# Latent attention on one core: VectorE copies the first tile's turned probabilities, and output products of finished heads are placed between the last steps

## What is computed

```
for j in range(S // Q_BLOCK):                       # 4 query tiles of 128 rows, S = 512
    L = (j + 1) * Q_BLOCK
    s = (q_nope[tile j] . k_nope[:L] + q_pe[tile j] . k_pe[:L]) * scale    # 16 heads
    p = softmax(where(causal_mask(...), s, NEG_INF))
    outs.append(einsum('bhqk,bkhd->bqhd', p, v[:, :L]))
o = concatenate(outs).reshape(B, S, 16 * 64)
x = x + g_m * (o @ w_o)                             # w_o is 1024 x 1024
x = x + g_f * hier_moe(...)                         # 32 experts, top 2 of one group
```

## Time and profile before

| | us |
|---|---|
| median of 3 runs | 1137.25 |
| lowest, highest | 1135.13, 1137.52 |
| the profiled execution, its own time | 1136.97 |
| its span in the trace | 1135.2 |
| around the span | 1.8 |

### The profile page before, as it was taken

One profiled execution on the slowest core, in us unless ns is written; L12 is line 12 of the kernel. 1 busy time (PEld: TensorE's weight loads), 2 busy tenths in 40 slices (PEclk: granted clock), 3 DMA queues, 4 the chain that ended last, 5 costly groups with the idle time before them and its releaser, 6 DMA issues.

```text
span 1135.2 us, 15295 instructions
## 1 busy us (share of the span) xinstructions
PE 1043.2 (92%) x5662; PEld 633.0 (56%) x5662; DVE 608.2 (54%) x1460; ACT 329.0 (29%) x896; POOL 92.1 (8%) x129
## 2 busy tenths in 40 slices
PE   4999999999998999897889999999998999979996
PEld 3444444656466666564556556655456656646652
DVE  6899989898646322221246577766235622222224
ACT  4321112875131111111124545666122121111110
POOL 1000000000011111111000000000000111201200
PEclk9999999999999999999999999999998999999999
DMA  9929868928568999999996300401826899999998
GB/s 368 405 79 392 332 259 328 420 83 347 190 270 340 409 417 419 418 418 420 417 396 261 124 1 38 149 1 61 334 88 259 311 420 420 418 414 418 419 416 351
DMA packets 66814, 341.44 MB, mean 301 GB/s; under 512 B 11110, under 2 KB 11366, under 8 KB 36400
## 3 DMA queue, kind: packets, MB, share of 16 engines
q1 hardware_dynamic: 49952, 297.68, 64.8%
q0 software_dynamic: 15120, 37.63, 8.5%
q10 hardware_dynamic: 1664, 5.09, 1.1%
HBM read 320.90 MB, written 37.24 MB: 315 GB/s over the span
## 4 chain that ended last, share of the span: by engine, by line
PE 75%; DMA 8%; SPq 5%; DVE 5%; ACT 3%; issue 3%; DVEq 0%; ACTq 0%; POOLq 0%
PE PP L928 16%; PE PP L694 12%; PE PP L804 10%; PE PP L943 8%; PE PP L716 3%; SPq L531 3%; DMA AHS<-in_moe_w 3%; PE PP L1145 3%; PE PP L667 2%; PE PP L1111 2%; PE PP L1149 2%; PE PP L901 2%; PE PP L753 2%; SPq L547 2%; PE PP L764 2%
## 5 line engine op out<-in xcount | busy, mean ns | idle before, releaser
L694 PE MATMUL PP<-ring,AHS 128*128 128x512 f32 x320 | 139.9, 592 | 0.0
L2028 DVE TENSOR_TENSOR PS<-PS,PP 128x256 f32<-128x256 f32 x33 | 13.9, 421 | 195.9 <-PE PP L928 186.3
L804 PE MATMUL PP<-ring,AHS 128*128 128x512 f32 x256 | 111.4, 593 | 0.8 <-ACT AHS L1491 0.8
L2035 DVE SCALAR_TENSOR_TENSOR PS<-PP,small,GF 128x512 f32<-128x512 f32 x66 | 46.5, 746 | 111.3 <-PE PP L943 100.7
L694 PEld LDWEIGHTS PP<-ring,AHS 128*128 128x128 f32 x320 | 59.7, 190 | 69.8 <-issue 69.8
L928 PE MATMUL PP<-RQK,RV 128*64 128x256 f32 x640 | 75.2, 392 | 10.5 <-issue 8.4
L804 PEld LDWEIGHTS PP<-ring,AHS 128*128 128x128 f32 x256 | 48.0, 190 | 58.4 <-issue 58.4
L928 PE MATMUL PP<-ring,RV 128*64 128x256 f32 (+1 forms) x608 | 75.5, 389 | 4.3 <-ACT RV L1525 1.7
L1549 ACT ACTIVATE PS<-PP 128x256 f32<-128x256 f32 x33 | 12.7, 384 | 217.1 <-PE PP L928 151.1
L928 PEld LDWEIGHTS PP<-RQK,RV 128*64 128x64 f32 x640 | 56.4, 142 | 32.1 <-issue 17.7
L928 PE MATMUL PP<-AHS,RV 128*64 128x256 f32 x640 | 71.9, 380 | 2.1 <-issue 2.1
(11 more groups left out here) (351 smaller groups left out, 1675.4 us busy)
## 6 DMA issues: line engine op xcount, KB each, us to landing
AHS<-in_moe_w SPq DMA_DIRECT2D x61, 1024.0 KB
ring<-in_moe_w SPq DMA_DIRECT2D x58, 1024.0 KB, 21.2
RQK<-in_moe_w SPq DMA_DIRECT2D x52, 1024.0 KB
ring<-in_ada_t SPq DMA_DIRECT2D x22, 1024.0 KB, 19.9
AHS<-in_ada_t SPq DMA_DIRECT2D x18, 1024.0 KB
X<-in_moe_w SPq DMA_DIRECT2D x16, 1024.0 KB, 23.3
ring<-in_da_w_qkv SPq DMA_DIRECT2D x10, 1024.0 KB, 13.8
RQK<-in_ada_t SPq DMA_DIRECT2D x8, 1024.0 KB
```

The lines of the kernel that those rows point to most:

```text
L694: last = mm(PB[qkv_bank(n)][:, :], HT[:, c, t * P:(t + 1) * P], us[c // 4][:, (c % 4) * NH:(c % 4 + 1) * NH], start=c == 0, stop=c == C - 1)
L804: last = mm(PB[2 * t + n][:, :], (OT, OTM)[l][:, k, t * P:(t + 1) * P], us[k // 2][:, (k % 2) * D + n * NH:(k % 2) * D + (n + 1) * NH], st ...
L2035: last = stt(ysb[b][:, cols], PB[5 + m][:, :], weight, GF[:, cols], ALU.mult, ALU.mult)
```

## The change

Three things are done.

1. The copy of a tile 0 step, both heads at once, is issued by VectorE and no longer by ScalarE. It stands where VectorE's copies of tiles 2 and 3 stand, after `maxima(i + 2)`. The waits on `tev` and `tev1` count accordingly. Tile 1 stays with ScalarE alone, and tiles 2 and 3 stay split.
2. Fourteen of tile 0's sixteen products with `w_o` are issued earlier. Of the first half (`n = 0`), chunk 0 stands between the values and the turn of step 29, chunk 1 between the values and the turn of step 31, chunk 2 behind that turn, chunks 3, 4, 5 and 6 behind the values of the last pair; then come chunks 0 to 6 of the second half. `project_out(1)` issues the two products of chunk 7 for tile 0 and the rest as before.
3. For these products TensorE waits earlier for the four transfers of `w_o` and for `omla` at 6 (both at the head of iteration 30), for the exponentials of step 30 (which read banks 0 and 1), and for `omla` at 7 before chunk 6.

Layer 0 computes `begun` in another way with the same values.

```
+def by_vector_alone(i):
+    return i % T == 0
+def by_both(i):
     return i % T >= 2
+def vector_copies(i):
+    return sum(by_vector_alone(j) or by_both(j) for j in range(i + 1))
+def scalar_copies(i):
+    return sum(not by_vector_alone(j) for j in range(i + 1))
...
@@ mla_turn
-                wait(pe, sem("tev"), i)
-                wait(pe, sem("tev1"), mla_copies(i - 1))
+                wait(pe, sem("tev"), scalar_copies(i - 1))
+                wait(pe, sem("tev1"), vector_copies(i - 1))
...
@@ mla_values
-                    pe.wait_ge(sem("tev"), 4 * g + 4)
-                    pe.wait_ge(sem("tev1"), mla_copies(4 * g + 3))
+                    pe.wait_ge(sem("tev"), scalar_copies(4 * g + 3))
+                    pe.wait_ge(sem("tev1"), vector_copies(4 * g + 3))
...
@@ project_out, product(t)
-                        begun = 1 if (l, t, n) == (0, 0, 0) else 0
+                        begun = 0 if t else C - 1 if l else 1 - n
...
@@ attend(i) on TensorE, between mla_values and mla_turn
+                    if i == 29:
+                        pe.wait_ge(sem("exp"), 32 + 31)
+                        mixed(1, 0, 0, wo, (0,))
+                    if i == 31:
+                        mixed(1, 0, 0, wo, (1,))
...
@@ the loop over the steps
+                    if i == 30:
+                        wo = [take(1, "wo", u) for u in range(4)]
+                        pe.wait_ge(sem("omla"), 6)
...
                 attend(31)
+                mixed(1, 0, 0, wo, (2,))
                 for k in range(T):
                     mla_values(7, k)
+                mixed(1, 0, 0, wo, (3, 4, 5))
+                pe.wait_ge(sem("omla"), 7)
+                mixed(1, 0, 0, wo, (6,))
+                mixed(1, 0, 1, wo, range(C - 1))
...
@@ ScalarE, mla_turned
+                if by_vector_alone(i):
+                    return
...
@@ VectorE, probabilities_out
+                    if by_vector_alone(i):
+                        v.tensor_copy(turned_pair(t), PP[2][:, :, 0:(t + 1) * P].rearrange("p a (k q) -> p a k q", k=t + 1)).then_inc(
+                            sem("tev1"), 1)
```

More of the change, by code:

```diff
@@ L128 @@
 ROOTS = {20: 0, 22: 1, 28: 2}
-def mla_on_vector(i):
+def by_vector_alone(i):
+    return i % T == 0
+def by_both(i):
     return i % T >= 2
-def mla_copies(i):
-    return sum(mla_on_vector(j) for j in range(i + 1))
+def vector_copies(i):
+    return sum(by_vector_alone(j) or by_both(j) for j in range(i + 1))
+def scalar_copies(i):
+    return sum(not by_vector_alone(j) for j in range(i + 1))
 def wait(eng, sem, value):
@@ L1361, in mla_turned @@
                 g, t = divmod(i, T)
+                if by_vector_alone(i):
+                    return
                 act.wait_ge(sem("tr"), 32 + i + 1)
                 wait(act, sem("av"), 32 + i - T + 1 if g else 0)
-                if mla_on_vector(i):
+                if by_both(i):
                     fn(turned(0, t), PB[4][:, 0:(t + 1) * P].rearrange("p (k q) -> p k q", k=t + 1),
@@ L2202, in probabilities_out @@
                     g, t = divmod(i, T)
-                    if mla_on_vector(i):
+                    if by_both(i) or by_vector_alone(i):
                         dve.wait_ge(sem("tr"), 32 + i + 1)
                         wait(dve, sem("av"), 32 + i - T + 1 if g else 0)
+                    if by_both(i):
                         v.tensor_copy(turned(1, t), PB[5][:, 0:(t + 1) * P].rearrange("p (k q) -> p k q", k=t + 1)).then_inc(
+                            sem("tev1"), 1)
+                    if by_vector_alone(i):
+                        v.tensor_copy(turned_pair(t), PP[2][:, :, 0:(t + 1) * P].rearrange("p a (k q) -> p a k q", k=t + 1)).then_inc(
                             sem("tev1"), 1)
```

## The result

The changed kernel took 1126.78 us, the median of five executions (1125.98 to 1129.95); the kernel before, five executions on the same chip, 1136.69 us (1132.06 to 1137.52). The ratio is 0.9926, with a 95% interval from 0.9901 to 0.9951. Faster was forecast, but 5.45 us of it, not 9.9, and 1126.8 lies under the range of 1129.8 to 1135.0. Two later groups of executions of the same two kernels gave 0.9951 (0.9935 to 0.9968) and 0.9949 (0.9932 to 0.9966). Two single executions that took 1826 and 3774 us are left out everywhere.

What follows compares the result with a forecast made beforehand. TensorE was taken to bound the attention and the product behind it, weight transfers the stage after. Holes worth 2.5 us and 2.9 us at the end gave 5.45 us before rounding, 1137.25 to 1131.8 us, range 1129.8 to 1135.0.

Steps and rivals of the forecast that it cites:

- The holes are ScalarE's tile 0 copy: Attention: TensorE's 0.38 us hole each 10.74 us is a tile 1 turn waiting for ScalarE's copy, queued behind exponentials.
- Part 1's size: Attention loop, copy moved to VectorE: the hole goes in each group, 0.2 + 2.33 us, together 2.5 without the last group.
- What is late next: Attention, turn 14: VectorE's longer queue delays ScalarE's tile 1 copy; 0.13 us of cover left, 0.8 us lost by upper bound.
- the start of ScalarE's tile 1 copy: Attention: ScalarE's copy of step 13 starts at 750.09 and not 749.86, as the exponentials start 0.23 us late.
- the rule that was weighed: Skill's rule: work either engine can do may better go to ScalarE when VectorE is saturated; then 1134.3 us, chance 0.12.
- Part 2's size: End of the attention: fourteen products of 0.866 us fill holes, gaining 0.94, 0.37, 0.83 and 0.78, together 2.92 us.
- the sign of being wrong that the prediction named: Between the turns at the attention's end: a product taking more than 0.87 us would show the prediction wrong.
- What reaches the end: Behind the last product: the saturated transfer stretch starts and ends 5.4 us earlier, with the same bytes left.
- The rival of hidden gains: Stage behind 889.60 us: transfers that could not start earlier hide the gain; 1137.2 us, no change, chance 0.06.
- The end time: Whole kernel: 1137.25 us less 5.45 gives 1131.8; the likeliest case, chance 0.78.
- 1 us of spread as in the runs: Term in the likeliest case's own range, 1130.3 to 1133.6, beside 0.8 for the copy and 0.7 for the waits.
- The clock: Routing, 858.90 to 889.60 us: a shifted clock fall slows the first pairs' matmuls; 1141.8 us at 10 us, chance 0.04.

Runs made afterwards that it cites:

- the double copy: The changed kernel with VectorE copying each tile 0 step a second time, to a place nobody reads: ratio 0.9953, beside 0.9949 for the changed kernel.
- 2.90 alone: The changed kernel with ScalarE copying tile 0 as before, so only the fourteen products placed earlier: ratio 0.9989 to the kernel before.
- the copy alone: The changed kernel without the early products, so only VectorE copying tile 0: ratio 0.997 to the kernel before.
- the short start: The changed kernel with 6 instead of 16 filler records at the start: ratio 0.9942; with 60 instead of 44 before layer 0's first gather too: 0.9921.

## Why the prediction was right and where it was wrong

- **The holes are ScalarE's tile 0 copy.** Right. The turns of tile 1 follow with no wait once VectorE does it, and a group takes (731.88 - 721.55) = 10.33 us in the changed kernel (turn 8 less turn 4, which starts at 721.55), forecast 10.35.
- **Part 1's size.** 2.5 us were forecast without the last group, 3.00 measured: from the first w_o transfer to the release of the buffers by the last scores it is 789.09 - 632.03 = 157.06 us before and 782.57 - 628.51 = 154.06 after. The mis-sized terms are small: 0.425 on the mean for a group where 0.39 was read (from turn 4 to turn 28 it is 64.48 us before and 61.93 after, six groups), and 0.45 up to turn 4 (the change's only hole there is the first, read as 0.2). Idle time in front of a matmul is read from the modelled end of the one ahead, and such ends overlap the next start: turn 9 above ends at 734.26 by its record, and the scores behind it start at 734.09.
- **What is late next.** The working had 0.13 us of cover before turn 14, and the double copy shows some 0.39. The step that failed is the start of ScalarE's tile 1 copy: it was put 0.88 us behind the start of the exponentials, as in the earlier trace rows (748.98 to 749.86). Part of that distance was ScalarE waiting for the turn, whose record ends at 749.82; after the change it is 0.70 (734.00 to 734.70). With exponentials that also start 0.08 us sooner than was worked out, the copy starts 2.82 us behind the start of turn 8, where the working had 3.08 (750.09 - 747.01). The wait did not change its engine, as it would have by the rule that was weighed: VectorE took the copy, and some 0.39 us more of it, almost for nothing.
- **Part 2's size.** 2.92 us forecast, 2.98 measured in the changed kernel (69.82 us from the last scores to the last product before, 66.84 after) and 2.90 alone. Each place can be checked by starts. From turn 28 to turn 29 it is 2.18 us before and 2.12 after with a product in between, so 0.06 + 0.866 = 0.93 is gained where 0.94 was forecast; from turn 31 to the last values 1.89 and 1.87, so 0.89 where 0.83 was forecast. The product before turn 29 adds 0.96 us and not 0.866: with the copy alone, turn 29 starts 1.16 us behind turn 28 (784.53 - 783.37), and 2.12 with the product. That is the sign of being wrong that the prediction named (more than 0.87 us between the turns), but it costs 0.1 us and no more.
- **What reaches the end.** Right: from the release to the end of the span it is 276.3 us before and 275.6 after, and 274.8 to 276.1 in the three later profiles of the two kernels. The rival of hidden gains is out.
- **The end time.** Wrong, 5.0 us too high. The forecast of 1131.8 was 1137.25 less 5.45. All executions of the kernel before here, 71, have a mean of 1134.8 us (1129.9 to 1138.5), and all 22 of the changed kernel 1128.8 (1126.0 to 1132.5); the difference is 6.1 us with a standard error of 0.5, which is the 5.98 of the traces. So of the 5.0 us, 2.4 are the median of three runs of before, taken as its level though it lies that much above the mean of 71; 0.6 are the size of the change; and 2.0 are the five executions of the changed kernel, whose median lies that much under the mean of 22. The step that failed is the range's term for scatter, "1 us of spread as in the runs", together with the median of three runs as the level it was laid on. Single executions scatter with a standard deviation of 1.9 us on either side, and medians of three and five move by one to two. The mechanism and its sum were right, and the first ratio, 0.9926, was by 0.0024 a lucky one.
- **The clock.** It was named as a rival for the routing of layer 1, on the slower side. It was at work in layer 0, ahead of the change, and in the faster direction for this pair of profiles: 1.4 us at the start, 1.7 around the first expert pair of layer 0, 0.5 further on. The two kinds of start do not make up all of the scatter between executions: the late profiles differ by 3.2 us among themselves at the w_o transfer, and part of that has no place and no cause here. How often each kind occurs in the executions without a profile is not known.

## What to carry to other kernels

A copy that frees a buffer should be queued on the engine that is idle when the buffer is full, not on the one that is less busy on average: here 0.42 us moved to the busier engine gained 0.42 us a group. Work that is ready and needs no wait (products of finished heads) is worth placing only where the loop runs out of cover, and there it pays what the holes were, no more. Before a change of half a per cent is believed, measure a fixed stretch of the trace around it (here it repeats to 0.01 us) and compare events ahead of the change: 3.5 us of the 10.2 were there already.

## What was not expected of the hardware

The same 16 records of filler after the same idle time took from 2.67 to 3.42 us in different executions, and the place of a later fall of the clock, 315 us further on, went with it: in the twelve profiles with the unedited start, the router's first filler took 6.2 to 6.7 us for 32 records in all seven in which those 16 had taken 3.41 or 3.42 us, and 0.12 us for each record in all five in which they had taken 2.67 to 2.91. Why, no run shows; in the two profiles with the short start (first filler 5.35 and 6.76 us) the order is another. A granted clock of 0.54 at the first expert pair came with 2.2 us of idle time ahead of it and not with 1.65 us or less. And a product of 512 columns put between two series of transposes moved the second by 0.96 us where it takes 0.866 in a row of its kind.
